# A tenth place for weight blocks, experts written out, and small reads moved between queues, in a two-layer decoder step

## What is computed

```python
pc = softmax(t @ w_coarse + b_coarse); pg, gidx = top_k(pc, 1)
fine_sel = take(einsum('td,gde->tge', t, w_fine) + b_fine, gidx)
vals, eidx = top_k(softmax(fine_sel), 2)          # two experts of the chosen group
for g in range(4):
    hid = silu(einsum('td,edf->tef', t, w_gate[g])) * einsum('td,edf->tef', t, w_up[g])
    out += einsum('tef,efd->td', hid * comb[:, g, :, None], w_down[g])
```

## Time and profile before

| | |
|---|---|
| median of 3 runs | 812.34 us |
| the profiled execution | 811.95 us |
| its span, first to last instruction | 810.1 us |
| mean granted TensorE clock | 0.957 |
| busy: TensorE / VectorE / ScalarE / GpSimd | 713.7 / 282.2 / 227.1 / 126.8 us |
| moved by DMA | 281.54 MB, mean 348 GB/s |

### The profile page before, as it was taken

One profiled execution on the slowest core, in us unless ns is written; L12 is line 12 of the kernel. 1 busy time (PEld: TensorE's weight loads), 2 busy tenths in 40 slices (PEclk: granted clock), 3 DMA queues, 4 the chain that ended last, 5 costly groups with the idle time before them and its releaser, 6 DMA issues.

```text
span 810.1 us, 22139 instructions
## 1 busy us (share of the span) xinstructions
PE 713.7 (88%) x9473; PEld 451.8 (56%) x9474; DVE 282.2 (35%) x703; ACT 227.1 (28%) x404; POOL 126.8 (16%) x211
## 2 busy tenths in 40 slices
PE   3999999899999999777787988988999999979682
PEld 1577887576555555444344557755555555545351
DVE  1139998831841212111111175157121211112017
ACT  1134667511612222211111243033122222212120
POOL 0090587700010101000000000000010101001000
PEclk9999999799999999999899999999999999989897
DMA  9999633798992999999999999999599999999941
GB/s 307 391 266 352 238 123 104 277 313 287 408 415 104 414 417 417 418 418 417 419 416 419 404 381 388 405 408 361 225 415 418 419 416 419 419 415 419 420 174 53
DMA packets 73454, 281.54 MB, mean 348 GB/s; under 512 B 4013, under 2 KB 4627, under 8 KB 57014
## 3 DMA queue, kind: packets, MB, share of 16 engines
q1 hardware_dynamic: 70690, 273.88, 86.4%
q0 software_dynamic: 2048, 5.86, 2.3%
q10 hardware_dynamic: 676, 1.24, 0.5%
HBM read 278.54 MB, written 3.37 MB: 348 GB/s over the span
## 4 chain that ended last, share of the span: by engine, by line
PE 60%; DMA 20%; DVE 9%; SPq 7%; ACT 2%; issue 2%; DVEq 0%; ACTq 0%
PE bank L751 16%; PE bank L760 7%; PE bank L1030 7%; PE bank L892 7%; SPq L488 6%; DMA ring<-in_w_up 6%; PE bank L730 5%; PE bank L789 5%; DMA ring<-in_w_in_even 4%; PE bank L597 4%; DMA ring<-in_w_down 3%; DMA big<-in_w_down 3%; DMA big<-in_w_up 3%; DVE t L1383 3%; DMA ring<-in_w_ada 2%
## 5 line engine op out<-in xcount | busy, mean ns | idle before, releaser
L751 PE MATMUL bank<-ring,big 128*32 128x256 f32 x2112 | 131.0, 401 | 27.7 <-DMA ring<-in_w_up 24.1
L1842 DVE SCALAR_TENSOR_TENSOR big<-big,bank 128x128 f32<-128x128 f32 x49 | 17.0, 347 | 319.0 <-ACT big L1325 319.0
L751 PEld LDWEIGHTS bank<-ring,big 128*32 128x32 f32 x2112 | 70.8, 115 | 82.5 <-DMA ring<-in_w_up 30.5
L1979 POOL TENSOR_TENSOR big<-t 128x192 f32<-128x192 f32 x51 | 26.4, 517 | 520.9 <-PE bank L730 393.0
L751 PE MATMUL bank<-big 128*32 128x256 f32 x1024 | 65.2, 408 | 18.6 <-DMA big<-in_w_up 15.0
L730 PE MATMUL bank<-htm,big 128*32 128x256 f32 x1224 | 77.2, 386 | 0.0
L1328 ACT ACTIVATE big<-bank 128x256 f32<-128x256 f32 x49 | 18.8, 383 | 205.1 <-PE bank L760 205.1
L892 PE MATMUL bank<-big,ring 128*128 128x264 f32 x320 | 74.1, 390 | 0.7 <-DMA ring<-in_w_in_even 0.7
L892 PEld LDWEIGHTS bank<-big,ring 128*128 128x128 f32 x320 | 59.9, 190 | 12.5 <-issue 1.9
L1325 ACT ACT_TABLE_LOAD x49 | 62.9, 1283 | 6.7 <-DVE chunk_table L1814 5.8
L760 PE MATMUL bank<-ring,big 128*32 128x256 f32 x1056 | 63.1, 379 | 1.7 <-DMA ring<-in_w_down 1.7
(11 more groups left out here) (259 smaller groups left out, 736.6 us busy)
## 6 DMA issues: line engine op xcount, KB each, us to landing
ring<-in_w_ada SPq DMA_DIRECT2D x24, 2048.0 KB, 15.5
ring<-in_w_gate SPq DMA_DIRECT2D x42, 1024.0 KB, 19.9
ring<-in_w_up SPq DMA_DIRECT2D x42, 1024.0 KB, 22.0
ring<-in_w_down SPq DMA_DIRECT2D x21, 2048.0 KB, 24.8
big<-in_w_gate SPq DMA_DIRECT2D x22, 1024.0 KB, 20.7
big<-in_w_up SPq DMA_DIRECT2D x22, 1024.0 KB, 21.7
big<-in_w_down SPq DMA_DIRECT2D x11, 2048.0 KB, 24.8
ring<-in_w_in_even SPq DMA_DIRECT2D x5, 2048.0 KB, 33.0
```

The source lines that it names most:

```text
L751: last = mm(GU[C * q:C * (q + 1), :].rearrange("p (a j i) -> p a j i", a=2, j=KF), hgc[:, C * k:C * (k + 1)], cols, start=(k == 0), stop=( ...
L1979: v.tensor_tensor(flat, all_r, all_b[:, :, bass.ds(g, 1)].broadcast_to([P, 2 * TT, C]), ALU.mult)\
```

## The change

A tenth place, `spare`, is added: 16 KB per partition. The descriptor scratch for GpSimd is set to 2048 bytes, and `lgt` is laid over constants that are no longer needed by then. `ring` and `big` become parts of one tile `arena`. An expert's three blocks now take the next three of ten places in turn, so they are not neighbours; the gate and up pair is read with a stride between two places, and whichever lies lower takes the gate matrix. Of the pair, the first is read whole, the second in halves. The first matrix of expert e+1 is asked for when expert e-3 has done its down product; (0,3,0) already before the second `out0` block, (1,3,0) before `fill_rest(1)`. The loop over groups of three experts is written out, so each layer has 16 bodies, and their waits are on constants. The 14 routing reads go from GpSimd to SyncE, ahead of `ada` 5. GpSimd asks for the states before the conv reads, and VectorE multiplies them at level 3 instead of 1. The rows of the last norm go to place 4, without a wait. Three semaphores are merged into others that have the same order. The diff, cut to its core:

```diff
-NSLOT = 9
+NSLOT = 10
-SETS = [[(4, 5, 0), (6, 7, 8), (1, 2, 3)], [(6, 7, 8), (0, 1, 2), (3, 4, 5)]]
+HOMES = [[4, 5, 0, 6, 7, 8, 1, 2, 3, 9], [6, 7, 8, 1, 5, 0, 3, 9, 4, 2]]
...
+    plan += [((0, e, i), HOMES[0][(3 * e + i) % NSLOT]) for e in range(2, EXPERTS) for i in range(3)]
+    plan += [(("ada", 15), 3), (("ada", 16), 9), (("ada", 17), 4), (("out1", 0), 5), (("out1", 1), 0), (("ada", 18), 1),
+             (("ada", 19), 2), (("ada", 20), 3), (("ada", 21), 9), ((1, 0, 0), 6), ((1, 0, 1), 7), (("ada", 22), 4),
+             ((1, 1, 0), 1), ((1, 1, 1), 5), (("ada", 23), 2), ((1, 1, 2), 0), ((1, 2, 0), 3), ((1, 2, 1), 9),
+             ((1, 0, 2), 8), ((1, 2, 2), 4)]
+    plan += [((1, e, i), HOMES[1][(3 * e + i) % NSLOT]) for e in range(3, EXPERTS) for i in range(3)]
...
-        ring = sb("ring", [P, RING, 4096])
+        BIG = 9152 + 128 + 3 * KD * T
+        arena = sb("arena", [P, 4096 * (RING + 1) + BIG])
+        spare = arena[:, 0:4096]
+        ring = arena[:, 4096:4096 * (RING + 1)].rearrange("p (s n) -> p s n", s=RING)
...
-        lgt = sb("lgt", [20, TT * P])
+        lgt = con[0:20, K_MASK + D:K_MASK + D + TT * P]
...
-        final_rows = ring[:, 0, 0:2 * D].rearrange("p (i n) -> p i n", i=2)
+        final_rows = ring[:, 4, 0:2 * D].rearrange("p (i n) -> p i n", i=2)
...
+        def gate_and_up(l, e):
+
+            a, b = sorted(at(SLOT[(l, e, i)]) for i in range(2))
+            whole = arena[:, :]
+            return bass.AP(whole.tensor, whole.offset + a, [whole.ap[0], (b - a, 2), (1, 4096)])
+
+        def expert_fills(l, e, n):
+
+            per_layer = len(range(e % n, EXPERTS, n))
+            return 16 * (l * per_layer + e // n + 1)
...
             def fill_expert(l, e, i):
 
-                if i < 2:
+                if i == 0:
+                    sp.dma_start(slot((l, e, i), KD), expert_unit(l, i, e)).then_inc(first_in[e % 4], 16)
+                elif i == 1:
                     for half in range(2):
-                        fill_half(l, e, i, half)
+                        fill_half(l, e, half)
                 else:
...
             def fill_rest(l):
 
                 sp.wait_ge(M[l]["table_ready"], l + 1)
                 for e in range(3, EXPERTS):
-                    chunks = sp.value_load(tab[l][0:1, e - 2:e - 1], min_val=1, max_val=MAXCH)
+                    chunks = through(l, e - 3)
                     for half in range(2):
                         sp.wait_ge(M[l][("gu_half", "gu_done")[half]], chunks)
-                        for i in range(2):
-                            fill_half(l, e, i, half)
+                        fill_half(l, e, half)
+                    fill_expert(l, e, 2)
                     sp.wait_ge(M[l]["down_done"], chunks)
-                    fill_expert(l, e, 2)
+                    if e < EXPERTS - 1:
+                        fill_expert(l, e + 1, 0)
 
             for name in ORDER[:ORDER.index(("ada", 12)) + 1]:
...
+                if name == ("out0", 1):
+                    fill_expert(0, 3, 0)
+                if name == ("ada", 5):
+                    for l in range(2):
+                        sp.dma_start(wr[:, l, :, 0:4], I["w_coarse"][l].rearrange("(k p) n -> p k n", p=P))\
+                            .then_inc(s_mix1, 16)
+                        for g in range(4):
+                            sp.dma_start(wr[:, l, :, 4 + 4 * g:8 + 4 * g],
+                                           I["w_fine"][l, g].rearrange("(k p) n -> p k n", p=P)).then_inc(s_mix1, 16)
+                        sp.dma_start(br[0:4, l:l + 1], I["b_coarse"][l:l + 1, :].rearrange("l n -> n l")).then_inc(s_mix1, 16)
+                        sp.dma_start(br[4:20, l:l + 1], I["b_fine"][l:l + 1].rearrange("l g e -> (g e) l"))\
+                            .then_inc(s_mix1, 16)
                 unit_free(sp, name)
                 fill(name)
...
             fill_rest(0)
...
+            fill(("ada", 15))
+            chunks13 = through(0, 13)
+            sp.wait_ge(M[0]["gu_done"], chunks13)
+            fill(("ada", 16))
+            fill(("ada", 17))
+            sp.wait_ge(M[0]["down_done"], chunks13)
+            fill(("out1", 0))
+            sp.wait_ge(M[0]["gu_done"], through(0, 14))
+            fill(("out1", 1))
...
+            for i in range(2):
+                unit_free(sp, (1, 2, i))
+                fill_expert(1, 2, i)
             sp.wait_ge(E("tm_tr"), 4 * TT)
             fill_expert(1, 0, 2)
-            for i in range(1, 3):
-                unit_free(sp, (1, 2, i))
-                fill_expert(1, 2, i)
+            unit_free(sp, (1, 2, 2))
+            fill_expert(1, 2, 2)
+            unit_free(sp, (1, 3, 0))
+            fill_expert(1, 3, 0)
             fill_rest(1)
-            chunks13 = sp.value_load(tab[1][0:1, EXPERTS - 2:EXPERTS - 1], min_val=1, max_val=MAXCH)
-            sp.wait_ge(M[1]["gu_done"], chunks13)
...
-                def expert(j, lo, hi, both_filled, filled):
+                def expert(e, lo, hi):
...
+                        pe.wait_ge(first_in[e % 4], expert_fills(l, e, 4))
+                        pe.wait_ge(second_in[e % 3], expert_fills(l, e, 3))
                         gate_up(wgu, range(KD // 2)).then_inc(m["gu_half"], 1)
-                        pe.wait_ge(gu_in2[j], both_filled)
+                        pe.wait_ge(second_in2[e % 3], expert_fills(l, e, 3))
...
-                with pe.Fori(0, EXPERTS // 3) as ep:
...
+                for e0 in range(0, EXPERTS, 3):
+                    n = min(3, EXPERTS - e0)
+                    word = pe.value_load(bounds[l][0:1, e0 // 3:e0 // 3 + 1], min_val=0, max_val=2 ** 24 - 1)
+                    b = [pe.snap(((word >> (6 * i)) & 63).with_bounds(min_val=0, max_val=MAXCH)) for i in range(n + 1)]
+                    for j in range(n):
+                        expert(e0 + j, b[j], b[j + 1])
...
-                if s == 1:
+                if s == 3:
                     dve.wait_ge(s_state, 32)
...
+            for a in range(2):
+                pool.dma_start(st4[:, :, a, :], I["state_gla"][0, :, 2 * a:2 * a + 2].rearrange("b h k v -> (h k) b v"))\
+                    .then_inc(s_state, 16)
...
-            for l in range(2):
-                pool.dma_start(wr[:, l, :, 0:4], I["w_coarse"][l].rearrange("(k p) n -> p k n", p=P))\
-                    .then_inc(s_mix1, 16)
...
-    nc = bacc.Bacc("TRN2", target_bir_lowering=False, num_devices=1)
+    nc = bacc.Bacc("TRN2", target_bir_lowering=False, num_devices=1, dynamic_dma_scratch_size=2048)
```

More of the change, by code:

```diff
@@ L352, in build @@
         final_s = af[0:NS, 0:D]
-        unit_in = [sem(f"slot_filled{i}") for i in range(NSLOT)]
-        gu_in, gu_in2, down_in = ([sem(f"{n}_in{j}") for j in range(3)] for n in ("gate_up", "gate_up_rest", "down"))
+        unit_in = {i: sem(f"slot_filled{i}") for i in range(NSLOT) if not RING <= i < NSLOT - 1}
+        first_in, down_in = ([sem(f"{n}_in{j}") for j in range(4)] for n in ("first_matrix", "down"))
+        second_in, second_in2 = ([sem(f"{n}_in{j}") for j in range(3)] for n in ("second_matrix", "second_matrix_rest"))
         s_out = sem("stored")
@@ L379, in held, with at, gate_first @@
         def held(s):
-            return ring[:, s, :] if s < RING else late[:, s - RING, :]
+            return ring[:, s, :] if s < RING else late[:, s - RING, :] if s < NSLOT - 1 else spare
+        def at(s):
+            return 4096 * (s + 1) if s < RING else 4096 * (RING + 1) + LATE0 + 4096 * (s - RING) if s < NSLOT - 1 else 0
+        def gate_first(l, e):
+            return at(SLOT[(l, e, 0)]) < at(SLOT[(l, e, 1)])
+        def gate_and_up(l, e):
[5 more added lines that the diff above has]
+            return 16 * (l * per_layer + e // n + 1)
         def slot(name, m):
@@ L472, in expert_unit @@
             def expert_unit(l, i, e):
-                name = ("w_gate", "w_up", "w_down")[i]
+                name = ("w_gate", "w_up", "w_down")[i if i == 2 or gate_first(l, e) else 1 - i]
                 w = I[name][l, e % 4, e // 4]
@@ L528, in _ @@
             fill_rest(0)
-            chunks14 = sp.value_load(tab[0][0:1, EXPERTS - 1:EXPERTS], min_val=1, max_val=MAXCH)
-            for i in range(3):
-                sp.wait_ge(M[0]["gu_done" if i < 2 else "down_done"], chunks14)
-                fill(("ada", 15 + i))
-            chunks15 = sp.value_load(tab[0][0:1, EXPERTS:EXPERTS + 1], min_val=1, max_val=MAXCH)
+            fill(("ada", 15))
[7 more added lines that the diff above has]
+            fill(("out1", 1))
+            chunks15 = through(0, 15)
             sp.wait_ge(M[0]["gu_done"], chunks15)
-            for i in range(2):
-                fill(("out1", i))
+            fill(("ada", 18))
             sp.wait_ge(M[0]["down_done"], chunks15)
-            fill(("ada", 18))
-            for i in range(19, 22):
+            fill(("ada", 19))
+            for i in range(20, 22):
                 unit_free(sp, ("ada", i))
@@ L804, in moe @@
                 pe.wait_ge(m["bounds_ready"], l + 1)
```

(2 more changed lines are left out.)

56 lines of the change are left out of this document (14 added, 42 removed).

## The result

The changed kernel took 800.93 us (median of 4, 799.69 to 801.18) beside 813.21 us (810.41 to 814.46) for the kernel before: ratio 0.9851 [0.9821, 0.988]. Its profiled execution took 801.04 us with a span of 799.2, so 10.9 us less span than before. The forecast was 802.3.

The account below looks back on a forecast made before the run. Transfers were taken to end both expert stages, with TensorE having time to spare. Terms -5.0 - 5.0 - 0.7 + 0.7 = -10.0 us gave 801.9 for the profiled execution, 802.3 for the median; range 797.9 to 809.5.

Parts of the forecast that it names:

- Tenth place: Both expert stages: one block asked for early, in idle transfer time, leaves 5.02 us less saturated transfer; gain 5.0 us per layer.
- Larger reads: First matrices of experts read at once in rows of 16 KB instead of 8: between 0 and 1 us gained, taken as 0.
- The hole before layer 1: Transfers rest from about 572 to 579 us; the extra 5.02 us block fits and shrinks this to some 2 us.
- rival 1: Only layer 0 gains, as block plus queue lag may fill the 7 us rest before layer 1: 807.3 us; chance 0.16.
- Written out: Expert stages: 24 more bodies add 0.29 MB of instruction reads in saturated stretches; 0.7 us lost.
- rival 4: Cold code stops TensorE 1.98 us at each of 13 further expert bodies per layer: 818.8 us; chance 0.03.
- Routing reads: Opening: fourteen small reads moved to SyncE no longer mix with the last w_in blocks, ending a TensorE wait; gain 0.7 us.
- the bound of 50 us: Upper price of ten moved reads on SyncE's queue, 5 us each; queue some 15 us behind at 165 us, half absorbed by holes.
- rival 3: Small scratch holds each GpSimd transfer until the one before has landed, a median 7.4 us for store ones; chance 0.05.
- States: States asked for first, their VectorE product of 2.35 us two levels later: nothing, between 2.4 us gained and 2.4 lost.
- Small scratch: GpSimd's descriptor space: one hold of 11 us in the opening and 7.4 us at the stores, both hidden; taken as 0.

Follow-up runs that it names:

- written_out_only: The kernel before, with nine places, changed only by writing the experts out as sixteen bodies a layer: 815.52 us, ratio 1.0052.

## Why the prediction was right, step by step

The total was right (-10.9 of span against -10.0; 800.93 us against 802.3) and so was the mechanism of the two large terms: transfers end the layers, and a block loaded into idle time is one block less behind the first refill. Several sizes were not right, and that they add up to nearly the forecast is partly luck.

- *Tenth place, -5.0 and -5.0: right in kind, and 3.2 to 4.9 in size.* Against the written-out kernel with nine places, stage 0 is 5.03 and stage 1 4.85 us shorter, but that holds more than the early request: taking only this request away costs 3.8 and 3.2. With loops, where hardly any rows are long, the tenth place is worth 4.9 and 4.0.
- *Larger reads, 0: too small.* The rate of 418 against 416 GB/s makes an estimated 0.9 us a layer, most of the 1.3 and 1.7 us that the kernel without the lead has over `written_out_only`. The rest, with the other order of refills, is not separated. That lead and long rows together come to the 5.0 us of one block is luck.
- *The hole before layer 1* held the block: rival 1 did not come.
- *Written out, +0.7: mis-sized.* It is 4.2 us [2.5, 5.8] by the times and 3.4 in the profile. I counted bytes: 45 reads expected (56 came), 0.29 MB over the full rate. By the landings above, half of the engines are not late and the latest is, by 2.5 and 2.7 us, and a landing needs the slowest; that single reads do this fits but is argued. The stop at first entries, rival 4, never showed. The Trainium skill ("Runtime: NRT & Kernel Launch", section Instruction fetch mechanics) prefers full unrolling; in this kernel the measured 1.0052 speaks against it, and no stop is seen at an entry.
- *Routing reads, -0.7: too small.* Alone 2.0 us. The 0.7 was read from a wait in an execution whose TensorE began 1.9 us late; begun on time, it waits 2.09 us for the same block. On SyncE the reads took from 58.39 to 80.1 us, mostly behind a full queue (the last four `w_fine` 2.59 us). The estimated 28 us from the Trainium skill's fixed part ("DMA: Bandwidth & Descriptors", section Anatomy of one DMA) would also have been hidden; the rows say 21.7. A slip in the bound of 50 us: by rival 3's own count the two holes take 18 us, so all of the 15 us and not half.
- *States, 0 within +-2.4:* 1.2 us lost alone, and 1.8 won by undoing the later product in the changed kernel; both are single profiles, and like executions differ by up to 0.9 us there.
- *Small scratch, 0: right only beside the routing move.* I bounded the stops at 11 and 7.4 us and found 7.75 and 9.81, the second above its bound, both hidden as argued. Rival 3, transfers that wait for each other, did not come at the stores; its like came in the opening as soon as the routing reads stayed on GpSimd. I wrote that only the two states have 1024 pieces; ten of the routing reads of the kernel before have as many, in the same queue, and what I missed is that the two edits are one. And it shortens the end by 1.5 to 1.9 us, which I said would be unchanged.
- *The clock of the first passes*, 1.7 and 1.6 us in the changed kernel's favour, was not forecast. In layer 0 four of six loop kernels (without the added products) show 3.66 us, as all written-out ones do. In layer 1 all six loop kernels take 5.10 to 5.35 and five of the six written-out ones 3.66. So in layer 1 the written-out form may have a part in it; no run isolates that, and what chooses is open.

As a sum of differences from the written-out kernel with nine places: +3.4 (that form, with its faster first passes and its 1.3 us between the layers), -1.4 (to layer 0), -5.0 (stage 0), -1.4 (between, mostly that kernel's clock), -4.9 (stage 1), -1.6 (rest) = -10.9.

## What to carry over

Where transfers saturate a stage, price an extra block of buffer that is loaded ahead of it by its bytes over the rate: 5.0 us here, of which the early request gave 3.2 to 4.9. When code grows, mind the slowest DMA engine and not only the bytes. Read a small wait in more than one execution before pricing what removes it. Cut a resource only after listing every transfer on that queue: here the same 2048 bytes cost nothing or some 17 to 21 us, depending on who sends fourteen tiny reads.

## What the runs showed of the chip that I had not expected

- With 56 instruction reads the landings of a layer's last requests spread over 2.8 to 5.9 us, with 28 over 1.8 to 2.5; one kernel with 29 has 2.6 to 3.5 in layer 0.
- A packet of 2, 4, 8 and 16 KB takes a median of 87, 161, 313 and 615 ns on its DMA engine: 16 KB rows gain 2% on 8 KB ones. An instruction read of 16 KB takes 1.08 us. The 10240 packets of 16 B take 9 ns each.
- With the small scratch GpSimd stops 1.6 to 7.1 us at each 1024-piece read of 16 KB, and the program ends 1.5 to 1.9 us sooner after its last store.
- SyncE itself stops when much is under way: in the kernel before a request takes 0.33 us at 577.96, and mostly 1.8 to 5.5 us from 644 us on (up to 7.9 in the changed kernel).
